# Latent attention: the mask is added by VectorE while it takes the row minimum into SBUF, and the transposes follow two tiles behind

## The chip, the cores and the metric

The kernel runs on one core of one Trainium2 chip. TensorE (PE) multiplies matrices from SBUF into PSUM; VectorE (DVE), ScalarE (ACT) and GpSimd (POOL) work beside it, each in the order of its own queue, and wait for one another through semaphores. The metric is the device time of one execution in microseconds, as the median of several runs.

## The reference, cut to what matters

The program runs four layers. The last two (`second_block`, one layer after the other) each hold a latent attention over 1024 tokens with 8 heads; this is what the change touches:

```python
def mla(q_lat, kv_lat, k_rope, ...):
    ...
    sc = (einsum('bqhd,bkhd->bhqk', qn, k_nope)       # 64 features a head
          + einsum('bqhd,bkd->bhqk', qp, k_pe)) * scale  # 32 rotated features, one key for all heads
    mask = key_chunk[None, :] <= q_chunk[:, None]     # chunks of 64 tokens
    sc = where(mask, sc, -inf)
    p = softmax(sc, axis=-1)
    return einsum('bhqk,bkhe->bqhe', p, v)
```

A query sees all keys of its own chunk of 64 and of the chunks before it. In a tile of 128 queries that leaves one corner to be hidden: the first 64 queries don't see the last 64 keys of the tile's own 128.

## The kernel before, in words

`latent_attention` is one stage between two barriers of all engines. It runs over 4 pairs of heads (p), and in each over 8 tiles of 128 queries (i); tile u = 8p + i has (i + 1) x 128 keys. The two heads of a pair are the two sides. The queries are scaled by a negative factor, so that the scores are negated, the row *minimum* is taken and the exponential is exp(minimum - score).

PSUM has 8 banks. Each side owns two banks for its scores (`s_bank`); a tile with i < 4 fills one of them (the even tiles the first, the odd ones the second), a longer one both. Three banks (`t_bank`) go round for transposes: each group of transposes takes the next bank and waits until the group three before it has been copied out (`begin`, `emptied`, `KEEP` = 3). The last bank gathers the values (`o_bank`).

All four score banks are held until the exponentials have read them: `scores` waits on "probs_ready". One step n of the loop on each engine is:

- PE: `scores(n)`: the 64-feature products (L3456), the rotated products (L3463), then for each side a product of one row by one row that adds 1e30 to the hidden corner (L3469, `early` and `late`). Then `turn(n-1)`: the probabilities of the tile before are transposed (L3484) in groups of up to four blocks. A long tile has the groups full0, full1 and then diag, or diag0 and diag1. Then pieces of other work: the queries of the next pair (`turn_q`, i = 2 and 4), the products with the values (`triangle_values`, `full_values`, L3489) and the spreading of the inverse sums (`spread`, L3510).
- DVE: a row minimum from PSUM for each side (L3603), then its share of copying out the groups (full1, diag1), the copies of the next pair's queries (i = 2 and 4: two, then four instructions), and at i = 0 and 5 the weighing of the output (`weigh`).
- ACT: copies out the first of its groups (full0), then takes the two exponentials (L3631, from PSUM to `probs`, with the row sums), then copies its other group (diag or diag0).

`probs` has two buffers. The order of all groups is written out in `LatentGroups.listed`.

The same form of instruction that the change brings in stands already in the neighbourhood attention of the first layer (L804): `tensor_tensor_reduce` from PSUM and an SBUF bias into `na_probs`, with exponentials in place behind it (L819).

Of the kernel before, what the change touches and what calls it, by code (L numbers as in the profile page):

```python
# [3327 lines left out]
class LatentGroups:  # L3328


    KEEP = 3

# [20 lines left out]
    def listed(self):  # L3353
        for part in range(4):
            yield ("q", 0, part), 1 - part % 2
        for n in range(4 * TILES + 8):
            p, i = divmod(n, TILES)
            if 1 <= n <= 4 * TILES:
                u = n - 1
                for a, what in enumerate(self.of_tile(u % TILES)):  # L3360
                    yield ("turn", u, what), 1 - a % 2
            if p < 3 and i in (2, 4):
                for part in range(2):
                    yield ("q", p + 1, (i - 2) + part), 0
            if 1 <= p <= 4 and i == 0:
                yield ("inv", p - 1, 0), 0
            if 1 <= p <= 4 and i == 5:
                yield ("inv", p - 1, 1), 0


def latent_attention(nc, core, Qn, Qr, knT, krT, V, gate, mixT):
# [9 lines left out]
    probs = [m.at("mla_probs", W + 62 * KB, [P, 2, SEQ]), m.at("mla_probs", W + 109 * KB, [P, 2, SEQ])]  # L3381
# [4 lines left out]
    low = m.at("mla_low", X + 30 * KB, [P, U, 2])  # L3386
    sums = m.at("mla_sums", X + 30 * KB + 256, [P, PAIRS_, 2, 2, 4])
    inv = m.at("mla_inv", X + 30 * KB + 512, [P, PAIRS_, 2, 2, 4])
    early = m.at("mla_early", X + 31 * KB, [P, P], F32R)
    late = m.at("mla_late", X + 31 * KB + 512, [P, P], F32R)  # L3390
# [10 lines left out]
    def scores_of(u, side):  # L3401

        i = u % TILES
        flat = s_bank[side].rearrange("p b n -> p (b n)")
        at = (i % 2) * BANK if i < 4 else 0
        return flat[:, at:at + (i + 1) * P]
    with stage(nc, "scores_ready", "lows_ready", "probs_ready", "groups_ready", "emptied_dve", "emptied_act", "inverted", "values_ready",
               "weighed", "masks_ready") as (block, s):
# [8 lines left out]
        def _(pe):  # L3417
# [18 lines left out]
            def scores(u):  # L3436
                p, i = divmod(u, TILES)
                if i == 0:
                    for part in range(4):
                        emptied(pe, ("q", p, part))  # L3440
                if u == 0:
                    pe.wait_ge(s["masks_ready"], 2)
# [7 lines left out]
                for b in range((i + 4) // 4):  # L3450
                    n = min(BANK, (i + 1) * P - b * BANK)
                    at = i % 2 if i < 4 else b
                    cols = slice(b * BANK, b * BANK + n)
                    for side in range(2):
                        rows = slice(side * NOPE, (side + 1) * NOPE)
                        pe.matmul(s_bank[side][:, at, 0:n], qnT[p % 2][rows, q], knT[rows, p, cols], start=True, stop=False)  # L3456
                for b in range((i + 4) // 4):
                    n = min(BANK, (i + 1) * P - b * BANK)
                    at = i % 2 if i < 4 else b
                    cols = slice(b * BANK, b * BANK + n)  # L3460
                    for side in range(2):
                        r0 = (2 * b + side) * ROPE
                        pe.matmul(s_bank[side][:, at, 0:n], qrT[p % 2][r0:r0 + ROPE, q], krT[r0:r0 + ROPE, cols],  # L3463
                                  start=False, stop=(b < i // 4))
                at = i % 2 if i < 4 else 1
# [5 lines left out]
                mm.then_inc(s["scores_ready"], 1)  # L3471

            def turn(u):
                i = u % TILES
                r = i % 4
                pe.wait_ge(s["probs_ready"], 2 * u + 2)
                for what in G.of_tile(i):
                    bank = begin(("turn", u, what))
                    sides = range(2) if what == "diag" else [int(what[-1])]
                    first, count = (0, 4) if what.startswith("full") else (i - r, r + 1)  # L3480
                    for a, side in enumerate(sides):
                        for k in range(count):
                            at = (a * count + k) * P
                            mm = pe.transpose(bank[:, at:at + P], probs[u % 2][:, side, (first + k) * P:(first + k + 1) * P], c["ident"])  # L3484
                    mm.then_inc(s["groups_ready"], 1)
# [30 lines left out]
            for n in range(U + 6):  # L3516
                p, i = divmod(n, TILES)
                if n < U:
                    scores(n)
                if 1 <= n <= U:  # L3520
                    turn(n - 1)
                if p < PAIRS_ - 1 and i in (2, 4):
                    for part in range(2):
                        turn_q(p + 1, (i - 2) + part)
                if p < PAIRS_ and i == 6:
                    tile_emptied(pe, n - 4)
                    tile_emptied(pe, n - 3)
# [7 lines left out]
                if p >= 1 and i == 1:  # L3535
# [4 lines left out]
                if p >= 1 and i == 2:  # L3540
                    full_values(p - 1, (2, 3))
                if p >= 1 and i == 3:
                    triangle_values(p - 1, 1, (0, 1))
                if p >= 1 and i == 4:
                    triangle_values(p - 1, 1, (2, 3)).then_inc(s["values_ready"], 1)
                if p >= 1 and i == 5:
                    spread(p - 1, 1)
# [35 lines left out]
        def _(dve):  # L3583
# [10 lines left out]
            dve.tensor_copy(early[:, :], c["early"]).then_inc(s["masks_ready"], 1)  # L3594
            dve.tensor_copy(late[:, :], c["late_big"]).then_inc(s["masks_ready"], 1)
            for part in (1, 3):
                copy_q(dve, 0, part)
            for n in range(U + 6):
                p, i = divmod(n, TILES)
                if n < U:  # L3600
                    dve.wait_ge(s["scores_ready"], n + 1)
                    for side in range(2):
                        dve.tensor_reduce(low[:, n, side:side + 1], scores_of(n, side), AX.X, ALU.min).then_inc(s["lows_ready"], 1)  # L3603
# [6 lines left out]
                if 1 <= n <= U:  # L3610
                    copy_turned(dve, n - 1, 0, slice(None))
# [3 lines left out]
                if p >= 1 and i in (0, 5):  # L3615
                    weigh(p - 1, i // 5)

        @block.scalar
        def _(act):
            for part in (0, 2):  # L3620
                copy_q(act, 0, part)
            for n in range(U + 1):
                p, i = divmod(n, TILES)
                if n >= 1:
                    copy_turned(act, n - 1, 1, slice(0, 1))
                if n < U:
                    for side in range(2):
                        act.wait_ge(s["lows_ready"], 2 * n + side + 1)
                        if n >= 2 and side == 0:
                            act.wait_ge(s["groups_ready"], G.number["turn", n - 2, G.of_tile((n - 2) % TILES)[-1]] + 1)  # L3630
                        act.activation(probs[n % 2][:, side, 0:(i + 1) * P], scores_of(n, side), ACT.Exp, bias=low[:, n, side:side + 1], scale=-1.0,  # L3631
                                       accum_out=sums[:, p, i // 4, side, i % 4:i % 4 + 1]).then_inc(s["probs_ready"], 1)
                if n >= 1:
                    copy_turned(act, n - 1, 1, slice(1, None))
# [305 lines left out]
```

## Time and profile before

| what | value |
|---|---|
| median of 3 runs | 3685.25 us (3684.77 to 3691.2) |
| span of the profiled execution | 3674.7 us, its clock 0.941 on average |
| median less that span | 10.55 us |
| PE / DVE / ACT busy, whole span | 90% / 52% / 38% |
| latent attention, first layer of the two | 2740.7 to 2909.9 us |
| latent attention, second layer of the two | 3403.1 to 3572.3 us |

The profiled execution has no time of its own beside its span; the three runs are other executions. Times within the profile are microseconds from the start of the span. Each fp32 product shows as two records on PE, each transpose as one. A duration that a timeline row gives for several instructions is that of the whole run of them; the ends on PE are modelled, so that what a piece of PE work takes is best read from its start to the start of the next one.

### The profile page before, as it was taken

The page shows a single profiled execution, that of the slowest core. Times are in us where ns is not written, and L with a number is a line of the kernel's source. Part 1 is how long each engine was busy: PE and PEld are TensorE (multiplying, and loading weights), DVE is VectorE, ACT ScalarE, POOL GpSimd, SP SyncE. Part 2 cuts the span into 40 slices and gives each one's busy share as a digit, 9 for nine tenths or more (in the row PEclk, how much of TensorE's full clock was granted, in tenths as well). Part 3 has the DMA queues.
Part 4 walks back from the last instruction along what each step waited for, and adds up shares of the span by engine and source line. Part 5 has one row for each costly group of instructions (what it writes and reads, how often), then busy time and mean ns, then how long its engine had stood idle before and what let it go on. Part 6 is the DMA issues. An engine that isn't in the chain of part 4 may idle for free. (4 is left out here: it accounts for less than half of the span.)

```text
span 3674.7 us, 49645 instructions
## 1 busy us (share of the span) xinstructions
PE 3313.7 (90%) x19127; PEld 2618.8 (71%) x19127; DVE 1919.2 (52%) x3346; ACT 1386.9 (38%) x2552; POOL 362.7 (10%) x295
## 2 busy tenths in 40 slices
PE   7999989799988989949799999799889989988899
PEld 6894457588876866737478888489755678975557
DVE  5525645566747735574547646623355443325554
ACT  2006651365744024433146646500254420024442
POOL 0100000233330000000023323100100000001000
PEclk9999989799999999969889999899789999978999
DMA  6517021587956410012358857511000221110003
GB/s 206 174 41 251 1 99 55 217 331 275 393 215 227 133 35 1 1 58 81 115 189 315 336 213 297 212 31 47 16 1 1 98 92 31 36 27 1 1 27 123
DMA packets 250401, 459.76 MB, mean 125 GB/s; under 512 B 45043, under 2 KB 120135, under 8 KB 249801
## 3 DMA queue, kind: packets, MB, share of 16 engines
q1 hardware_dynamic: 231753, 389.70, 30.1%
q0 software_dynamic: 18432, 67.12, 4.8%
q8 instruction: 143, 2.34, 0.3%
q14 instruction: 73, 0.60, 0.0%
HBM read 380.72 MB, written 73.33 MB: 124 GB/s over the span
## 5 line engine op out<-in xcount | busy, mean ns | idle before, releaser
L1774 PE MATMUL psum<-high_in,e_rowsT_high 128*128 128x256 f32 (+1 forms) x1080 | 330.3, 324 | 5.4 <-DVE e_rowsT_low L174 5.4
L1775 PE MATMUL psum<-high_in,e_rowsT_low 128*128 128x256 f32 (+1 forms) x1080 | 326.4, 320 | 0.0
L174 POOL TENSOR_TENSOR low_down<-w_down,high_out 128x1024 fp32r<-128x1024 f32 x64 | 195.5, 3071 | 312.8 <-ACT high_out L1852 312.8
L1774 PEld LDWEIGHTS psum<-high_in,e_rowsT_high 128*128 128x128 f32 x1080 | 206.7, 191 | 22.4 <-issue 6.1
L1775 PEld LDWEIGHTS psum<-high_in,e_rowsT_low 128*128 128x128 f32 x1080 | 207.0, 192 | 16.2
L3603 DVE TENSOR_REDUCE mla_low<-psum 128x1 f32<-128x256 f32 (+7 forms) x128 | 91.0, 753 | 145.7 <-PE psum L3469 145.7
L174 DVE TENSOR_TENSOR low_gate<-w_gate,high_in 128x1024 fp32r<-128x1024 f32 x128 | 148.0, 1218 | 6.5 <-ACT high_in L1852 6.5
L174 DVE TENSOR_TENSOR low_up<-w_up,high_in 128x1024 fp32r<-128x1024 f32 x128 | 148.0, 1218 | 0.0
L1852 ACT ACTIVATE high_in<-w_gate 128x1024 fp32r<-128x1024 f32 x128 | 124.8, 1058 | 60.4 <-issue 60.4
L1852 ACT ACTIVATE high_out<-w_down 128x1024 fp32r<-128x1024 f32 x128 | 124.8, 1050 | 18.8 <-DMA w_down<-in_exp_w_down 18.7
L1779 PE MATMUL psum<-low_up,e_rowsT_high 128*128 128x256 f32 x720 | 130.4, 283 | 0.0
L1852 ACT ACTIVATE high_in<-w_up 128x1024 fp32r<-128x1024 f32 x128 | 124.6, 1053 | 0.0
L1911 POOL COPY e_index<-moe_ids 128x1 uint32 (+1 forms) x49 | 9.5, 195 | 1154.3 <-POOLq L84 525.9
L156 ACT ACTIVATE proj<-psum 128x512 f32<-128x512 f32 (+2 forms) x32 | 16.9, 528 | 269.7 <-PE psum L308 229.6
L156 ACT ACTIVATE mla_probsT<-psum 128x512 f32<-128x512 f32 (+2 forms) x96 | 52.1, 543 | 173.8 <-PE psum L3484 173.8
L1798 PE MATMUL psum<-high_out,e_hiddenT_high 128*128 128x512 f32 x360 | 115.2, 401 | 0.0
L1801 PE MATMUL psum<-low_down,e_hiddenT_high 128*128 128x512 f32 x360 | 111.6, 391 | 0.0
L158 DVE COPY proj<-psum 128x512 f32<-128x512 f32 (+2 forms) x32 | 19.3, 603 | 176.4 <-PE psum L308 176.0
L1804 PE MATMUL psum<-high_out,e_hiddenT_low 128*128 128x512 f32 x360 | 111.1, 390 | 0.0
L308 PE MATMUL psum<-ring_high,s_x_low 128*128 128x512 f32 (+3 forms) x576 | 110.7, 334 | 0.0
L302 PE MATMUL psum<-ring_high,s_x_high 128*128 128x512 f32 (+3 forms) x576 | 110.7, 334 | 0.0
L306 PE MATMUL psum<-ring_low,s_x_high 128*128 128x512 f32 (+3 forms) x576 | 110.6, 334 | 0.0
(602 smaller groups left out, 7916.9 us busy)
## 6 DMA issues: line engine op xcount, KB each, us to landing
w_gate<-in_exp_w_gate SPq DMA_DIRECT2D x32, 2048.0 KB, 9.9
w_up<-in_exp_w_up SPq DMA_DIRECT2D x32, 2048.0 KB, 14.7
w_down<-in_exp_w_down SPq DMA_DIRECT2D x32, 2048.0 KB, 21.9
ada<-in_ada_w SPq DMA_DIRECT2D x24, 1024.0 KB, 7.9
expert_rows<-e_out POOLq DMA_DIRECT2D x47, 512.0 KB, 7.1
expert_rows<-zero_row SPq DMA_DIRECT2D x33, 512.0 KB, 7.0
token_rows<-x SPq DMA_DIRECT2D x32, 512.0 KB, 2.6
x<-token_rows SPq DMA_DIRECT2D x24, 512.0 KB, 6.7
```

The lines of the kernel that those rows point to most:

```text
L174: return eng.tensor_tensor(low, whole, high, ALU.subtract)
L302: pe.matmul(dst, lhsT, rhs, start=(m == 0), stop=False)
L306: pe.matmul(dst, lhsT, rhs, start=False, stop=False)
L308: mm = pe.matmul(dst, lhsT, rhs, start=False, stop=(m == len(ops) - 1))
L1774: pe.matmul(dst, rows_high[:, k, :], w_high[:, k, cols], start=(k == 0), stop=False)
L1775: pe.matmul(dst, rows_low[:, k, :], w_high[:, k, cols], start=False, stop=False)
L1779: mm = pe.matmul(dst, rows_high[:, k, :], w_low[:, k, cols], start=False, stop=(k == KT - 1))
L1798: pe.matmul(dst, hid_high[:, k, :], w_high[:, k, cols], start=(k == 0), stop=False)
L1801: pe.matmul(dst, hid_high[:, k, :], w_low[:, k, cols], start=False, stop=False)
L1804: mm = pe.matmul(dst, hid_low[:, k, :], w_high[:, k, cols], start=False, stop=(k == HT - 1))
L1852: act.activation(high(e, j)[:, k:k + STEP[j], :], W[e % 2][j][:, k:k + STEP[j], :], ACT.Copy).then_inc(s["w_high_ready"], 1)
L3603: dve.tensor_reduce(low[:, n, side:side + 1], scores_of(n, side), AX.X, ALU.min).then_inc(s["lows_ready"], 1)
```

## The change

- **The mask.** The two one-row products of each tile (L3469) go. A tile `mask` of 128 x 512 is set to zero and its last 128 columns get 1e30 for the first 64 rows. VectorE adds it while it takes the minimum.
- **The minimum.** `tensor_reduce` over a side's whole row is replaced by one `tensor_tensor_reduce` for each bank ("piece"): it reads the bank and the mask, writes the sum to `probs` in SBUF and gives the minimum. A piece without hidden columns reads one zero, broadcast. Tiles with i >= 4 have two pieces a side, and one small minimum over both (`low`, waited for by ACT through "lows_ready").
- **The score banks.** A bank is free as soon as VectorE has read it ("reduced"), not after the exponentials. PE waits for the piece two before.
- **The exponentials** read `probs` in SBUF and write it in place.
- **The lag.** `probs` has three buffers; `turn`, its copies, the values, the spreading and the weighing all come one step later. In the code this is `LAG = 2` and the shifted conditions.

```diff
 class LatentGroups:
     KEEP = 3
+    LAG = 2
...
-            if 1 <= n <= 4 * TILES:
-                u = n - 1
+            if self.LAG <= n < 4 * TILES + self.LAG:
+                u = n - self.LAG
...
-            if 1 <= p <= 4 and i == 0:
+            if 1 <= p <= 4 and i == 1:
                 yield ("inv", p - 1, 0), 0
-            if 1 <= p <= 4 and i == 5:
+            if 1 <= p <= 4 and i == 6:
...
+    def pieces_of_row(u):
+        i = u % TILES
+        return [(i % 2, 0, (i + 1) * P)] if i < 4 else [(0, 0, BANK), (1, BANK, (i - 3) * P)]
...
     scores(u), PE:
-                if i >= 4 or i == 0:
-                    if u >= 1:
-                        pe.wait_ge(s["probs_ready"], 2 * u)
-                else:
-                    if u >= 2:
-                        pe.wait_ge(s["probs_ready"], 2 * (u - 1))
+                pieces = pieces_of_row(u)
+                for b, (at, k0, n) in enumerate(pieces):
+                    if pieces_before(u) + b >= 2:
+                        pe.wait_ge(s["reduced"], 2 * (pieces_before(u) + b - 1))
...
-                for side in range(2):
-                    r0 = (2 * (i // 4) + side) * ROPE
-                    row = slice(r0, r0 + 1)
-                    mm = pe.matmul(s_bank[side][:, at, (i % 4) * P:(i % 4 + 1) * P], early[row, :], late[row, :],
-                                   start=False, stop=True)
...
     loop, PE (the turned tile and all that follows it, one step later):
-                if 1 <= n <= U:
-                    turn(n - 1)
+                if G.LAG <= n < U + G.LAG:
+                    turn(n - G.LAG)
...
-                if p < PAIRS_ and i == 6:
+                if p < PAIRS_ and i == 7:
...
                     triangle_values(p, 0, (0, 1, 2))
-                if p < PAIRS_ and i == 7:
-                    triangle_values(p, 0, (3,)).then_inc(s["values_ready"], 1)
                 if p >= 1 and i == 0:
+                    triangle_values(p - 1, 0, (3,)).then_inc(s["values_ready"], 1)
+                if p >= 1 and i == 1:
                     spread(p - 1, 0)
...
     DVE:
+            def reduce_row(u):
+                i = u % TILES
+                if u >= NP:
+                    dve.wait_ge(s["groups_ready"], G.number["turn", u - NP, G.of_tile((u - NP) % TILES)[-1]] + 1)
+                for b, (at, k0, n) in enumerate(pieces_of_row(u)):
+                    dve.wait_ge(s["scores_ready"], pieces_before(u) + b + 1)
+                    for side in range(2):
+                        hidden = mask[:, 0:1].to_broadcast([P, BANK]) if k0 + n < (i + 1) * P else mask[:, BANK - n:BANK]
+                        dst = low[:, u, side:side + 1] if i < 4 else part_low[:, u, side, b:b + 1]
+                        dve.tensor_tensor_reduce(probs[u % NP][side][:, k0:k0 + n], s_bank[side][:, at, 0:n], hidden,
+                                                 1.0, 3.0e38, ALU.add, ALU.min, dst).then_inc(s["reduced"], 1)
+                if i >= 4:
+                    dve.wait_ge(s["reduced"], 2 * pieces_before(u + 1))
+                    dve.tensor_tensor(low[:, u, :], part_low[:, u, :, 0], part_low[:, u, :, 1], ALU.min).then_inc(s["lows_ready"], 1)
...
     ACT:
-            for n in range(U + 1):
+            for n in range(U + G.LAG):
                 p, i = divmod(n, TILES)
-                if n >= 1:
-                    copy_turned(act, n - 1, 1, slice(0, 1))
+                if n >= G.LAG:
+                    copy_turned(act, n - G.LAG, 1, slice(0, 1))
                 if n < U:
                     for side in range(2):
-                        act.wait_ge(s["lows_ready"], 2 * n + side + 1)
...
+                        row = probs[n % NP][side][:, 0:(i + 1) * P]
+                        act.activation(row, row, ACT.Exp, bias=low[:, n, side:side + 1], scale=-1.0,
                                        accum_out=sums[:, p, i // 4, side, i % 4:i % 4 + 1]).then_inc(s["probs_ready"], 1)
-                if n >= 1:
-                    copy_turned(act, n - 1, 1, slice(1, None))
+                if n >= G.LAG:
+                    copy_turned(act, n - G.LAG, 1, slice(1, None))
```

## Rows read from the trace of the kernel before

**Rows 1.** The page's head: the span.

```profile
span 3674.7 us, 49645 instructions
```

**Rows 2.** Busy time by stretch: the stage in both layers, then pair 1.

```profile
core 0: us, PE busy (x) PEld busy (x) DVE busy (x) ACT busy (x) POOL busy (x), PEclk, DMA share, GB/s
2740.70:2909.92 169.22, 153.63 (x1296) 95.23 (x1296) 86.94 (x138) 72.24 (x177) 0.00 (x0) 1.00 0.00 1
3402.00:3573.00 171.00, 153.63 (x1296) 95.26 (x1297) 87.73 (x140) 73.25 (x179) 0.00 (x0) 1.00 0.00 1
...
2775.15:2816.96 41.81, 38.95 (x328) 24.10 (x329) 22.63 (x36) 17.90 (x45) 0.00 (x0) 1.00 0.00 1
```

**Rows 3.** Who waited for whom, 2740 to 2911 us (total, times, longest).

```profile
PE psum L3456 <- ACT mla_probs L3631: 13.3, 16, 1.8
...
PE psum L3484 <- ACT mla_probs L3631: 0.8, 1, 0.8
...
PE psum L3489 <- DVE mla_tmp L3589: 0.4, 1, 0.4
```

**Rows 4.** Timeline of pair 1's last two tiles: start, duration, instruction, idle before.

```profile
2806.63 1.53 PE L3484 MATMUL psum<-consts,mla_probs 128*128 128x128 f32 x12
...
2810.07 1.99 PE L3456 MATMUL psum<-mla_knT,mla_qnT 64*128 64x512 f32 x8 [0.45 <-ACT mla_probs L3631]
2811.99 1.14 PE L3463 MATMUL psum<-mla_krT,mla_qrT 32*128 32x512 f32 x8
2812.56 0.63 PE L3469 MATMUL psum<-mla_late,mla_early 1*128 1x128 f32 x2
2813.12 1.89 PE L3484 MATMUL psum<-consts,mla_probs 128*128 128x128 f32 x14
2813.22 2.35 DVE L3603 TENSOR_REDUCE mla_low<-psum 128x1 f32<-128x1024 f32 x2 [3.68 <-PE psum L3469]
2813.81 0.60 ACT L156 ACTIVATE mla_probsT<-psum 128x512 f32<-128x512 f32 x1 [3.31 <-PE psum L3484]
2814.48 1.11 ACT L3631 ACTIVATE mla_probs<-psum,mla_low 128x1024 f32<-128x1024 f32 x1
2814.94 1.09 PE L3489 MATMUL psum<-mla_probsT,mla_v 128*64 128x128 f32 x16
...
2815.61 1.11 ACT L3631 ACTIVATE mla_probs<-psum,mla_low 128x1024 f32<-128x1024 f32 x1
...
2816.72 0.48 ACT L156 ACTIVATE mla_probsT<-psum 128x384 f32<-128x384 f32 x1
2816.96 0.49 PE L3456 MATMUL psum<-mla_knT,mla_qnT 64*128 64x128 f32 x4 [0.93 <-ACT mla_probs L3631]
...
2817.86 0.88 PE L3484 MATMUL psum<-consts,mla_probs 128*128 128x128 f32 x6
```

**Rows 5.** Neighbourhood attention, first layer: L804 and L819 (ns min/median/max).

```profile
L804 DVE CUSTOM_DVE_ANT_0 na_probs<-psum,na_bias x96: 683/691/693, 280.2 to 476.3; 128x512 f32<-128x512 f32 x96
L804 DVE DVE_READ_ACCUMULATOR2_ANT na_low<- x96: 81/82/84, 280.8 to 476.9; 128x1 f32 x96
...
L819 ACT ACTIVATE na_probs<-na_probs,na_low x96: 705/722/724, 280.9 to 477.0; 128x512 f32<-128x512 f32 x96
```

**Rows 6.** Groups with their shapes apart, 2740 to 2911 us.

```profile
L3631 ACT ACTIVATE mla_probs<-psum,mla_low 128x512 f32<-128x512 f32 x8 | 5.4, 684 | 0.0
L3603 DVE TENSOR_REDUCE mla_low<-psum 128x1 f32<-128x512 f32 x8 | 5.2, 686 | 11.2 <-PE psum L3469 11.2
...
L3603 DVE TENSOR_REDUCE mla_low<-psum 128x1 f32<-128x128 f32 x8 | 2.0, 286 | 5.3 <-PE psum L3469 5.3
...
L3606 DVE RECIPROCAL mla_inv<-mla_sums 128x8 f32<-128x8 f32 x4 | 0.8, 192 | 0.0
```

**Rows 7.** The same view, 2600 to 2740 us: an operand broadcast along the row.

```profile
L3304 DVE TENSOR_TENSOR proj<-proj,mla_ms 128x1024 f32<-128x1024 f32 x1 | 1.2, 1226 | 0.0
```

**Rows 8.** Timeline of pair 0: the copies of the next queries.

```profile
2755.74 2.78 DVE L159 TENSOR_SCALAR mla_qrT<-psum 64x512 f32<-64x512 f32 x4
```

More of the change, by code:

```diff
@@ L3380, in latent_attention @@
     qrT = [m.at("mla_qrT", W + 28 * KB, [P, SEQ]), m.at("mla_qrT", X + 26 * KB, [P, SEQ])]
-    probs = [m.at("mla_probs", W + 62 * KB, [P, 2, SEQ]), m.at("mla_probs", W + 109 * KB, [P, 2, SEQ])]
+    probs = [[m.at("mla_probs", at, [P, SEQ]) for at in pair] for pair in
+             ((W + 62 * KB, W + 66 * KB), (W + 109 * KB, W + 113 * KB), (core.const_end - 4 * KB, core.const_end + 4 * KB))]
+    NP = len(probs)
     TRI = 10 * P
@@ L3385, in latent_attention @@
     tmp = m.at("mla_tmp", W + 74 * KB, [P, BANK])
[L3386 to L3390, printed above, removed]
+    low = m.at("mla_low", W + 76 * KB, [P, U, 2])
+    sums = m.at("mla_sums", W + 76 * KB + 256, [P, PAIRS_, 2, 2, 4])
+    inv = m.at("mla_inv", W + 76 * KB + 512, [P, PAIRS_, 2, 2, 4])
+    part_low = m.at("mla_part_low", W + 117 * KB, [P, U, 2, 2])
+    mask = m.at("mla_mask", X + 30 * KB, [P, BANK])
     s_bank = [core.psum[:, 0:2, :], core.psum[:, 2:4, :]]
@@ L3399, in triangle, with pieces_before, combined_before @@
         return r * (r + 1) // 2 * P
-    def scores_of(u, side):
+    def pieces_of_row(u):
         i = u % TILES
[L3404 to L3408, printed above, removed]
+        return [(i % 2, 0, (i + 1) * P)] if i < 4 else [(0, 0, BANK), (1, BANK, (i - 3) * P)]
+    def pieces_before(u):
+        p, i = divmod(u, TILES)
+        return 12 * p + (i if i < 4 else 4 + 2 * (i - 4))
+    def combined_before(u):
+        p, i = divmod(u, TILES)
+        return 4 * p + max(i - 4, 0)
+    with stage(nc, "scores_ready", "mask_steps", "reduced", "lows_ready", "probs_ready", "groups_ready", "emptied_dve", "emptied_act", "inverted", "values_ready",
+               "weighed") as (block, s):
         def emptied(eng, key):
@@ L3454, in scores @@
+                for b, (at, k0, n) in enumerate(pieces):
+                    if pieces_before(u) + b >= 2:
+                        pe.wait_ge(s["reduced"], 2 * (pieces_before(u) + b - 1))
                     for side in range(2):
                         rows = slice(side * NOPE, (side + 1) * NOPE)
[L3456 to L3460, printed above, removed]
+                        pe.matmul(s_bank[side][:, at, 0:n], qnT[p % 2][rows, q], knT[rows, p, k0:k0 + n], start=True, stop=False)
@@ L3461, in scores @@
+                for b, (at, k0, n) in enumerate(pieces):
                     for side in range(2):
                         r0 = (2 * b + side) * ROPE
-                        pe.matmul(s_bank[side][:, at, 0:n], qrT[p % 2][r0:r0 + ROPE, q], krT[r0:r0 + ROPE, cols],
-                                  start=False, stop=(b < i // 4))
-                at = i % 2 if i < 4 else 1
-                for side in range(2):
-                    r0 = (2 * (i // 4) + side) * ROPE
-                    row = slice(r0, r0 + 1)
-                    mm = pe.matmul(s_bank[side][:, at, (i % 4) * P:(i % 4 + 1) * P], early[row, :], late[row, :],
-                                   start=False, stop=True)
@@ L3471, in scores @@
-                mm.then_inc(s["scores_ready"], 1)
+                        mm = pe.matmul(s_bank[side][:, at, 0:n], qrT[p % 2][r0:r0 + ROPE, q], krT[r0:r0 + ROPE, k0:k0 + n],
+                                       start=False, stop=True)
+                    mm.then_inc(s["scores_ready"], 1)
             def turn(u):
@@ L3483, in turn @@
                             at = (a * count + k) * P
-                            mm = pe.transpose(bank[:, at:at + P], probs[u % 2][:, side, (first + k) * P:(first + k + 1) * P], c["ident"])
+                            mm = pe.transpose(bank[:, at:at + P], probs[u % NP][side][:, (first + k) * P:(first + k + 1) * P], c["ident"])
                     mm.then_inc(s["groups_ready"], 1)
@@ L3515, in _ @@
                 turn_q(0, part)
-            for n in range(U + 6):
+            for n in range(U + 7):
                 p, i = divmod(n, TILES)
@@ L3539, in _ @@
                     full_values(p - 1, (0, 1))
-                if p >= 1 and i == 2:
+                if p >= 1 and i == 3:
                     full_values(p - 1, (2, 3))
-                if p >= 1 and i == 3:
+                if p >= 1 and i == 4:
                     triangle_values(p - 1, 1, (0, 1))
-                if p >= 1 and i == 4:
+                if p >= 1 and i == 5:
                     triangle_values(p - 1, 1, (2, 3)).then_inc(s["values_ready"], 1)
-                if p >= 1 and i == 5:
+                if p >= 1 and i == 6:
                     spread(p - 1, 1)
@@ L3592, in weigh @@
                 dve.tensor_tensor(mixT[:, p, cols], tmp[:, :], t_bank(("inv", p, half)), ALU.mult).then_inc(s["emptied_dve"], 1)
-            dve.tensor_copy(early[:, :], c["early"]).then_inc(s["masks_ready"], 1)
-            dve.tensor_copy(late[:, :], c["late_big"]).then_inc(s["masks_ready"], 1)
+            def reduce_row(u):
[12 more added lines that the diff above has]
+                    dve.tensor_tensor(low[:, u, :], part_low[:, u, :, 0], part_low[:, u, :, 1], ALU.min).then_inc(s["lows_ready"], 1)
+            dve.memset(mask[:, :], 0.0).then_inc(s["mask_steps"], 1)
             for part in (1, 3):
                 copy_q(dve, 0, part)
-            for n in range(U + 6):
+            dve.wait_ge(s["mask_steps"], 1)
+            dve.tensor_copy(mask[0:CHUNK_2, BANK - P:BANK], c["late_big"][0:CHUNK_2, :]).then_inc(s["mask_steps"], 1)
+            dve.wait_ge(s["mask_steps"], 2)
+            for n in range(U + 7):
                 p, i = divmod(n, TILES)
                 if n < U:
-                    dve.wait_ge(s["scores_ready"], n + 1)
-                    for side in range(2):
-                        dve.tensor_reduce(low[:, n, side:side + 1], scores_of(n, side), AX.X, ALU.min).then_inc(s["lows_ready"], 1)
+                    reduce_row(n)
                 if p < PAIRS_ and i == 6:
@@ L3609, in _ @@
                     dve.reciprocal(inv[:, p - 1, 1, :, :], sums[:, p - 1, 1, :, :]).then_inc(s["inverted"], 1)
-                if 1 <= n <= U:
-                    copy_turned(dve, n - 1, 0, slice(None))
+                if G.LAG <= n < U + G.LAG:
+                    copy_turned(dve, n - G.LAG, 0, slice(None))
                 if p < PAIRS_ - 1 and i in (2, 4):
@@ L3614, in _ @@
                         copy_q(dve, p + 1, (i - 2) + part)
-                if p >= 1 and i in (0, 5):
-                    weigh(p - 1, i // 5)
+                if p >= 1 and i in (1, 6):
+                    weigh(p - 1, i // 6)
         @block.scalar
```

17 lines of the change are left out of this document (6 added, 11 removed).

## The prediction

> **What bounds the kernel now.** The change lives in two stages of some 170 us each, the latent attention of the last two layers; nothing outside them is touched, so I read those stretches only. The busy times by stretch come first [rows 2]. In the first layer's stage, from the first score product to the last output write, PE is busy 153.6 of 169.2 us at a granted clock of 1.00, DVE 86.9, ACT 72.2, and no transfer is under way. The second layer's stretch shows the same 153.63 us of PE. So PE sets the time, and what there is to win is its idle 15.6 us a layer and whatever work is taken off it. The waits say what the idle is made of [rows 3]: 13.3 us in 16 waits of the score products (L3456) for ACT's exponentials, 0.8 us of the last transposes for the last exponentials, 0.4 us of the values for the weighing. That is 14.5 us.
>
> The timeline of pair 1's last tiles shows how such a wait arises [rows 4]. Tile 7's scores are done when DVE starts at 2813.22. DVE needs 2.35 us for two minima, ACT takes the exponentials at 2814.48 and 2815.61, and only then are the banks free for the next scores, at 2816.96. PE meanwhile has the transposes of tile 6 and some values, and runs dry 0.93 us before. Pair 1 takes 41.8 us and has 2.86 us of such idle in all.
>
> **The change part by part.**
>
> *The mask products off PE.* Tile 7's pair of them starts at 2812.56 while the rotated products still stream; tiles 4 to 6 have theirs beside the rotated products of another bank. Sixteen transposes of 128 columns follow one another at (1.89 - 0.33)/14, some 0.11 us each [rows 4]. The two mask products have as many columns and run side by side, so together they cost at most 0.11 us, at least nothing, and I take 0.055. They are uncovered in five tiles of eight: 20 x 0.055 = 1.1 us a layer (0 to 2.2).
>
> *The new minimum.* The same instruction stands in the neighbourhood attention: 691 ns for 128x512 from PSUM with an SBUF operand, then 82 ns of accumulator read that the next instruction overlaps [rows 5]. The old minimum of that shape takes 686 ns, at 128 columns 286 [rows 6], so about 153 ns is fixed. A multiplication by an operand broadcast along the row takes 1226 ns for 1024 columns [rows 7], so the broadcast zero should cost nothing. A tile with i < 4 costs what it did. A long one pays the fixed part twice more and a small minimum over the pieces, which I price as the reciprocal, 0.19 us [rows 6], with some 0.1 us of waiting for the accumulator. That adds about 0.4 us for each of 16 tiles, 6.4 us a layer on DVE, which then has 93 of 169 us: no bound by sum.
>
> The Trainium skill ("VectorE: DVE Perf Modes", the section on the TRN2 errata) prices an SBUF-to-SBUF operation at 58 cycles plus its columns, 0.06 us for the small minimum; by it the sum would fall by about 1.3 us over both layers. The row of the reciprocal decides here.
>
> *The exponentials from SBUF.* 722 ns against 684 from PSUM at 512 columns [rows 5, 6]: 0.04 us more each, 0.08 a tile. But for a long tile ACT now starts only when both sides and the small minimum are done: for tile 7 that is 4 pieces at about 0.61, plus 0.3, plus 0.1 to begin with, so 2.9 us after the scores, where it was 1.4 (2813.12 to 2814.48).
>
> *The banks freed by DVE.* PE's wait for a score bank now ends when DVE has read the piece two before. After tile 7 that is 1.3 us, not 3.8 (2813.12 to 2816.96). PE has between two score blocks the transposes and more, so the 13.3 us go, except in one place. In pair 0 at i = 4 the DVE still has four copies of the next queries in front of it, 2.78 us [rows 8], and no values lie on PE yet to cover them. The step times, counted from tile 0's start: a product block takes 0.21 us and 0.214 for each 128 columns (1.92 for tile 7's L3456, twice 0.42 for tile 0), the rotated one at most that of 512, so scores 0 to 6 take 0.85, 1.28, 1.7, 2.1, 2.3, 2.55 and 2.8; a group of transposes takes 0.11 a block and some 0.15 once. Scores 4 then end at 10.3. DVE takes 1.65 and 0.3 for tile 4, copies one group of tile 2 (0.55) and then the four queries, and reads tile 5 only at 15.7. PE has transposes (tile 2, queries, tile 3) and scores 5, 5.2 us, to 15.5; scores 6 get their first bank at 15.7 + 1.2 + 0.1 = 17.0. Stall: 1.5 us, and 0.1 more at scores 4.
>
> *The lag, and the ring of three.* Transposes of tile n - 2 never wait for exponentials any more, but they do wait for the three transpose banks, and ACT copies the last group of a tile only behind the exponentials. I followed the steps of a steady pair with these durations, and 1.0 us for spreading, 1.9 for each half of the full values. From scores 2 at 0 on, the scores of tiles 3 to 7 and 0 begin at 4.9, 9.4, 14.4, 19.5, 24.7 and 30.7; DVE is done with tiles 2 to 7 at 2.8, 8.4, 13.8, 19.3, 24.9 and 30.5, ACT's exponentials at 3.8, 9.5, 15.5, 21.2, 27.1 and 32.9. Everything is ready when PE comes to it, with margins of 0.2 us and up, except at i = 0. From the end of scores 7, ACT's exponentials begin at +2.9, last 2 x 1.17, and end at +5.2. The copy of tile 5's diag group, four blocks (0.60), is done at +5.8. Tile 6's third group needs that bank, so it starts at +5.9. PE has as cover: transposes of tile 5 and the values, from 2806.63 to 0.45 before 2810.07, 2.99 us; scores 0, 0.85 us (2816.96 to 2817.86 less the mask); and two groups of four transposes, 0.86 [rows 4]. That is 4.75 with one hand-over, so PE stalls 1.15 us. The fourth group needs tile 6's first one copied, which ACT does next, by +6.4: another 0.25 us. So 1.4 us at this place, where 0.93 stood.
>
> It comes after tile 7 of pairs 0, 1 and 2: 4.2 us. After pair 3 there are no scores 0 to cover 0.85 of it: 2.25 us. With 1.6 us in pair 0 and 0.4 us in the tail, where the values still wait for the weighing, the new stalls are 8.45 us a layer.
>
> *At no cost.* The zeroing and copying of `mask` at the stage's start lie under the transposes and copies of the first queries, before any scores; if that cover were gone, two instructions of at most 0.7 us (by the 691 ns of 512 columns) [rows 5] would stand there once a layer. The three buffers and the longer loop issue nothing more; the same groups, values and weighings move one step down, and PE does them in the tail as before. No DMA is issued or moved.
>
> **The sum.** A layer gains 14.5 - 8.45 + 1.1 = 7.15 us; both 14.3. The profiled execution goes from its span of 3674.7 [rows 1] to 3660.4 us. The median of the runs is 10.55 us above that span, so I predict 3671 us.
>
> **The rivals.**
>
> *All idle goes.* If ACT's copies come sooner than I reckon, or PE's other work covers them, a layer wins 14.5 + 1.1, both 31 us: 3654 us. For it speaks that one step of lag is worth 5 to 6 us of PE work; against it the +5.9 to 4.75 above, of which none is a guess larger than 0.3 us. The Trainium skill ("Perfetto Trace Analysis", Optimizing Tensor Performance) advises to rotate independent groups through PSUM banks, so that their evacuation overlaps the next products; by this rule freeing the score banks alone would bring that 31 us. It doesn't bear on who empties the transposes' ring.
>
> *Nothing measurable.* The places with margins of 0.2 to 0.6 us (tile 7's fourth group at i = 1, tile 5's second and third at i = 7) turn into stalls of about 0.5 us too: three a pair, twelve a layer, 6 us of the 7.15. Then 3683 us. Against it: the steady tiles of before repeat to 0.01 us, so nothing jitters.
>
> *Slower: a dear minimum.* The instruction has been seen at one shape, 512 columns with a full second operand. If the pieces with broadcast or short operands run at half its rate, the four pieces of tile 7 take 2.4 us more, all of it on the chain scores, minimum, exponentials, copy, transpose; those of tiles 5 and 6 1.8 and 2.1. The stalls at i = 0 grow by 2.4 each (9.6 a layer), and i = 6 and 7 open by about 1.3 a pair (5): 14.6 - 7.15 = 7.5 us a layer lost, 3700 us. It decides from about 1.5 us more on that chain, 0.37 us a piece. Against it: the 5 ns between 691 and 686, and the broadcast row [rows 5 to 7].
>
> **How the numbers follow.** Forecast 0.56, all idle gone 0.14, nothing measurable 0.2, slower 0.1. The likeliest is 3671 us. The range has to reach to the second and third cases: 3655 to 3685 leaves out the slower one and little more. A measurement of this kernel tells about 0.2%, 7.4 us, from no change. Faster by more takes the first two and a little of the third: 0.74. Within: 0.17. Slower: 0.09.
>
> **What would show it.** The waits of L3456 for the exponentials gone; waits of L3456 for DVE's new instruction only in pair 0, near 1.5 us. Transposes (L3484) waiting for ACT's copies into `mla_probsT` once a pair, some 1.2 us and 0.25. New minima of 0.69 us at 512 and 0.29 at 128 columns; DVE near 93 us a stage; PE busy about 152.5 of 162. Exponentials of 512 columns at 0.72. I'd be wrong if the new instruction's short or broadcast form is dearer than the row of 512, if a held bank stops PE at more places than i = 0, or if PE's pieces take longer in their new order.

## The result and the profile after

The changed kernel takes 3659.4 us (median of 6 runs, 3655.2 to 3670.1), the kernel before in the same sets of runs 3681.7 us. The ratio is 0.995, with a 95% interval of 0.9936 to 0.9964: some 18 us faster, between 13 and 24 (the two medians lie 22.3 us apart). The forecast was 14.3 us.

What the change is worth is better read inside the two stages, whose lengths agree between the two layers to 0.01 us in both kernels. From here on the **stage** is the latent attention from the first score product to the end of the last output write. First the busy times by stretch of the changed kernel: the stage in the first layer, in the second, and pair 1.

```profile
core 0: us, PE busy (x) PEld busy (x) DVE busy (x) ACT busy (x) POOL busy (x), PEclk, DMA share, GB/s
2738.71:2899.18 160.47, 152.71 (x1232) 89.32 (x1232) 93.60 (x283) 75.23 (x177) 0.00 (x0) 1.00 0.01 1
3390.59:3551.06 160.47, 152.71 (x1232) 89.32 (x1232) 93.61 (x283) 75.23 (x177) 0.00 (x0) 1.00 0.01 1
2766.03:2805.69 39.66, 38.59 (x314) 22.66 (x312) 24.29 (x74) 18.58 (x44) 0.00 (x0) 1.00 0.01 1
```

Both stages went from 169.2 to 160.47 us [rows 2], together 17.5 us less. Pair 1 went from 41.81 to 39.66. The spans of the two profiles, 3674.7 and 3653.5, lie 21.2 us apart; the 3.7 us that the stages don't explain lie in parts that the change doesn't touch, and single runs of one kernel scatter by more than that.

Next the waits of the first layer's stage: who waited for whom, total, times, longest.

```profile
PE psum L3476 <- ACT mla_probsT L156: 4.7, 4, 1.6
...
PE psum L3457 <- DVE mla_part_low L3596: 1.7, 2, 1.4
...
PE psum L3481 <- DVE mla_tmp L3581: 0.5, 1, 0.5
```

The 13.3 us of score products waiting for exponentials [rows 3] are gone. PE waits in two new places: four times before transposes (L3476) for ACT's copies of earlier groups, and twice before scores (L3457) for DVE. With 0.5 us for the weighing that is 6.9 us against 14.5, so the waits give 7.6 of the 8.7 us that a layer gains. The other 1.1 us are about what the mask's products took (experiment 3).

The timeline around the end of pair 1 shows the first of the new waits (start, duration, instruction, idle before).

```profile
2802.77 1.53 PE L3476 MATMUL psum<-consts,mla_probs 128*128 128x128 f32 x12
2802.98 0.69 DVE L3596 CUSTOM_DVE_ANT_0 mla_probs<-psum,mla_mask 128x512 f32<-128x512 f32 x1 [0.89 <-PE psum L3461]
...
2804.23 1.53 PE L3481 MATMUL psum<-mla_probsT,mla_v 128*64 128x128 f32 x24
...
2805.55 0.16 DVE L3600 TENSOR_TENSOR mla_low<-mla_part_low 128x2 f32<-128x2 f32 x1
...
2805.69 0.49 PE L3457 MATMUL psum<-mla_knT,mla_qnT 64*128 64x128 f32 x4
2805.75 1.15 ACT L3641 ACTIVATE mla_probs<-mla_probs,mla_low 128x1024 f32<-128x1024 f32 x1 [1.69 <-DVE mla_low L3600]
...
2806.53 1.09 PE L3476 MATMUL psum<-consts,mla_probs 128*128 128x128 f32 x8
...
2806.90 1.13 ACT L3641 ACTIVATE mla_probs<-mla_probs,mla_low 128x1024 f32<-128x1024 f32 x1
...
2808.03 1.06 ACT L156 ACTIVATE mla_probsT<-psum 128x512 f32<-128x512 f32 x2
...
2808.66 1.03 PE L3476 MATMUL psum<-consts,mla_probs 128*128 128x128 f32 x6 [1.03 <-ACT mla_probsT L156]
...
2809.14 0.31 PEld L3476 LDWEIGHTS psum<-consts,mla_probs 128*128 128x128 f32 x3 [0.18 <-ACT mla_probsT L156]
...
2809.61 1.09 PE L3481 MATMUL psum<-mla_probsT,mla_v 128*64 128x128 f32 x16
```

Read it from the scores of tile 7, done at 2802.77. ACT starts its first exponential only at 2805.75, 3.0 us later, and is free at 2808.03, 5.3 us after the scores. Then it copies two groups in a row: tile 5's last and tile 6's first. PE transposed eight blocks of tile 6 from 2806.53 on and stood until the first of these copies was out: 1.03 us. A second, shorter stop is hidden inside the last group of six: the weight load for its fourth block (the PEld row at 2809.14) waited 0.18 us for the second copy. From the first of the fourteen transposes to what follows them takes 3.08 us here (2806.53 to 2809.61) and 1.92 us in experiment 8, which has no stop there. So the place costs 1.16 us, somewhat more than its wait row says.

The groups with their shapes apart, in the same stage, give the prices.

```profile
L3596 DVE CUSTOM_DVE_ANT_0 mla_probs<-psum,mla_mask 128x512 f32<-128x512 f32 x48 | 30.9, 688 | 37.9 <-PE psum L3461 37.8
...
L3641 ACT ACTIVATE mla_probs<-mla_probs,mla_low 128x512 f32<-128x512 f32 x8 | 5.7, 710 | 0.0
...
L3596 DVE CUSTOM_DVE_ANT_0 mla_probs<-psum,mla_mask 128x128 f32<-128x128 f32 x16 | 4.0, 287 | 2.3 <-PE psum L3461 2.3
...
L3600 DVE TENSOR_TENSOR mla_low<-mla_part_low 128x2 f32<-128x2 f32 x16 | 2.6, 161 | 0.6
```

### The profile page after: what moved, and what is told of

Read it like the earlier page. It is cut to its first block and busy times, and to the rows that moved or that the text cites. A ratio compares the mean times of both kernels' runs of the same rounds, so it can differ in the third digit from the quotient of the medians.

```text
span 3653.5 us, 49677 instructions
## 1 busy us (share of the span) xinstructions
PE 3304.2 (90%) x18999; PEld 2599.5 (71%) x18999; DVE 1933.3 (53%) x3634; ACT 1392.5 (38%) x2552; POOL 360.9 (10%) x295
## 5 line engine op out<-in xcount | busy, mean ns | idle before, releaser
L3596 DVE CUSTOM_DVE_ANT_0 mla_probs<-psum,mla_mask 128x512 f32<-128x512 f32 (+2 forms) x192 | 96.9, 555 | 99.3 <-PE psum L3461 99.1
L3641 ACT ACTIVATE mla_probs<-mla_probs,mla_low 128x256 f32<-128x256 f32 (+7 forms) x128 | 97.9, 766 | 47.9 <-DVE mla_low L3600 45.3
```

Source lines behind the costliest of these rows:

```text
L3641: act.activation(row, row, ACT.Exp, bias=low[:, n, side:side + 1], scale=-1.0, accum_out=sums[:, p, i // 4, side, i % 4:i % 4 + 1]).then_i ...
```

## The experiments

All start from the changed kernel, with the edits shown, and all are read by the stage of the first layer (160.47 us for the changed kernel). Four of them take the gain apart, four go after the stalls that are left.

**1. The banks held until the exponentials.** The lag of two tiles stays, but the scores wait as before:

```diff
 def scores(u):
+    if i >= 4 or i == 0:
+        if u >= 1:
+            pe.wait_ge(s["probs_ready"], 2 * u)
+    else:
+        if u >= 2:
+            pe.wait_ge(s["probs_ready"], 2 * (u - 1))
```

> The changed kernel, except that the score products of a tile again wait for the exponentials of the tile before (for the short tiles 1 to 3: of two tiles before), as in the kernel before. The measure is the length of the first layer's latent attention, from the first score product to the last output write: 169.2 us before, 160.5 changed. If the early release of the banks is what took PE's waits away, each long tile now stalls by chain less cover: tile 4 about 0.5 us, 5: 1.2, 6: 1.6, 7: 2.4, the next tile 0: 2.3, some 8 us a pair against 1.0 now, so about 188 us and a kernel near 3713 us. If the lag of two tiles alone brought the gain, the stage stays at 160 to 164 us.

The kernel takes 3757.7 us, the stage 211.05. The busy times of that stage:

```profile
2739.37:2950.42 211.05, 170.57 (x1232) 98.61 (x1232) 93.58 (x283) 75.90 (x177) 0.00 (x0) 0.90 0.00 1
```

And the end of pair 1 in its timeline, start, duration, instruction, idle before:

```profile
2818.32 1.77 PE L3463 MATMUL psum<-mla_knT,mla_qnT 64*128 64x512 f32 x8 [1.68 <-ACT mla_probs L3647]
...
2826.01 1.99 PE L3463 MATMUL psum<-mla_knT,mla_qnT 64*128 64x512 f32 x8 [2.50 <-ACT mla_probs L3647]
...
2834.60 0.59 PE L3463 MATMUL psum<-mla_knT,mla_qnT 64*128 64x128 f32 x4 [2.61 <-ACT mla_probs L3647]
...
2835.85 2.91 PE L3482 MATMUL psum<-consts,mla_probs 128*128 128x128 f32 x14
```

The stalls of this pair are the expected ones: 0.22 and 1.42 at tiles 4 and 5, then 1.68, 2.50 and 2.61 us, where 0.5, 1.2, 1.6, 2.4 and 2.3 were worked out. With the banks held, the rest of the change is thus worse than the kernel before. This run has the lag and the new minimum together, whose pieces make the exponentials come later; no run has the lag with the old minimum. But the stage is 23 us longer than expected. Some 4.5 us of it are more stalls than reckoned (39.5 us in all), and some 18 go with the clock. The granted clock is 0.90 over this stage, not 1.00, and PE's busy time for the same 1232 instructions is 170.6 us, not 152.7. The last row shows it: 14 transposes in 2.91 us after a stall, where the kernel before took 1.89 [rows 4].

**2. A lag of one tile**, the banks still freed by DVE:

```diff
-    LAG = 2
+    LAG = 1
...
-                if p < PAIRS_ and i == 7:
-                    tile_emptied(pe, n - 5)
-                    tile_emptied(pe, n - 4)
+                if p < PAIRS_ and i == 6:
+                    tile_emptied(pe, n - 4)
+                    tile_emptied(pe, n - 3)
...
-                if p >= 1 and i in (1, 6):
-                    weigh(p - 1, i // 6)
+                if p >= 1 and i in (0, 5):
+                    weigh(p - 1, i // 5)
```

(and so on for all conditions that the change had shifted).

> The changed kernel with the transposes one tile behind again, and all that follows them as before; the banks are still freed by the minimum. If the banks bring the gain and the lag only moves the last stall, transposes of tile 7 wait for the exponentials: chain 5.2 us, cover 3.75, 1.6 us for three pairs and 2.4 after the last, with about 2 us in pair 0: a stage of about 163 us against 160.5. If the lag is what carries the gain, the stage is at 169 us or above.

3667.5 us in one run, the stage 164.22 us, 164.26 in the second layer. The transposes wait five times for exponentials:

```profile
PE psum L3476 <- ACT mla_probs L3641: 7.6, 5, 2.5
...
PE psum L3457 <- DVE mla_qrT L159: 1.6, 1, 1.6
...
PE psum L3457 <- DVE mla_part_low L3596: 0.9, 1, 0.9
```

(The middle row stands before the stage.) Of the 8.7 us that a layer gains, 5.0 come without the second tile of lag (the mask's products are in them), and the second tile brings 3.7. By the rows of waits, 8.5 us here against 6.9, it should bring 1.6. The rest is in the main the clock. At the end of pair 2 the same 16 transposes that take 2.00 us elsewhere took 3.60 (the rows stand in the last section), and over the stage's last 14 us the granted clock was 0.88. By the starts of the instructions the two places lose some 3 us. What the second tile of lag saves at full clock is then nearer 1 us a layer than 3.7, an estimate from these times.

**3. The mask back on PE**, every minimum with a broadcast zero:

```diff
+                    if last:
+                        for side in range(2):
+                            r0 = (2 * b + side) * ROPE
+                            mm = pe.matmul(s_bank[side][:, at, (i % 4) * P:(i % 4 + 1) * P], early[r0:r0 + 1, :], late[r0:r0 + 1, :],
+                                           start=False, stop=True)
...
-                        hidden = mask[:, 0:1].to_broadcast([P, BANK]) if k0 + n < (i + 1) * P else mask[:, BANK - n:BANK]
+                        hidden = mask[:, 0:1].to_broadcast([P, n])
```

> The changed kernel with the mask's one-row products back on PE and a broadcast zero as the operand of every minimum. By my price of 0.055 us in five tiles of eight the stage grows by 1.1 us, from 160.5 to 161.6 us (2.2 us at most). If the products cost the time that their own records show (0.3 to 0.6 us a tile), it grows by 6 us or more. The minima with broadcast operands throughout keep their durations (0.69 us at 512 columns, 0.29 at 128) if a broadcast costs nothing.

3660.3 us in one run; the stage is 162.83 us, 2.4 more. But up to the scores of the last tile it is 0.78 us behind (139.41 against 138.63 us from the stage's start), 0.17 in each steady pair. The other 1.6 us fall in the tail, behind the last product of the mask. Its busy times, to be set against 1.00 in the same stretches of the changed kernel:

```profile
2737.00:2877.00 140.00, 134.80 (x1108) 81.76 (x1108) 83.07 (x258) 67.90 (x162) 0.00 (x0) 1.00 0.01 1
2877.00:2890.00 13.00, 11.38 (x96) 7.95 (x93) 6.91 (x19) 7.44 (x14) 0.00 (x0) 0.91 0.01 2
2890.00:2901.00 11.00, 9.29 (x98) 6.61 (x96) 4.16 (x7) 0.61 (x2) 0.00 (x0) 0.95 0.00 0
```

The 0.8 us are what is left after a stall has absorbed a part. Pair 1's end in this run:

```profile
2805.15 0.49 PE L3459 MATMUL psum<-mla_knT,mla_qnT 64*128 64x128 f32 x4
...
2806.06 1.09 PE L3486 MATMUL psum<-consts,mla_probs 128*128 128x128 f32 x8
...
2808.06 1.03 PE L3486 MATMUL psum<-consts,mla_probs 128*128 128x128 f32 x6 [0.91 <-ACT mla_probsT L156]
```

Scores 0 take 0.91 us to the next transposes, 0.84 in the changed kernel (2805.69 to 2806.53), and the stall behind them is 0.91 us in place of 1.03. Step by step, tiles 0 to 3 and 7 are each 0.06 to 0.07 us longer than in the changed kernel, tiles 4 to 6 not at all. So the mask's products cost PE some 1.2 us a layer, within 0 to 2.2 and near the 1.1 taken. The minima keep their times, 688 ns at 512 columns and 288 for 287 at 128: a broadcast operand costs nothing.

**4. A dear minimum.** A second, unused minimum in front of each piece:

```diff
+                        dve.tensor_reduce(again[:, u, side, b:b + 1], s_bank[side][:, at, 0:n], AX.X, ALU.min)
                         dve.tensor_tensor_reduce(probs[u % NP][side][:, k0:k0 + n], s_bank[side][:, at, 0:n], hidden,
```

> The changed kernel with a second, unused row minimum in front of each piece, so that each piece costs about twice as much on DVE (0.6 us more at 512 columns, 0.2 at 128). This is the price that the prediction gave to its slower case: 14.6 us a layer more than forecast, a stage of about 175 us and a kernel slower than before. DVE's sum would then be near 135 us, still less than the stage, so a view by busy sums alone expects under 165 us.

3733.2 us, the stage 195.02 us: slower than before by 26 us a layer, and 20 us more than the 175 expected. Its waits:

```profile
PE psum L3458 <- DVE mla_part_low L3598: 14.3, 18, 3.1
...
PE psum L3477 <- DVE mla_probsT L158: 6.7, 4, 2.3
...
PE psum L3477 <- ACT mla_probsT L156: 6.0, 4, 1.6
```

DVE is busy 137 of 195 us, so no sum of busy times would show a bound, and PE still stalls 29 us, 22 more than in the changed kernel where 14.6 were expected. The expectation counted the exponentials' chain only. It missed that PE now waits 18 times for DVE to free a score bank, and for DVE's own copies too. PE's busy time is 12 us longer besides, of which the granted clock of 0.95 accounts for some 10.

**5. ACT copies first.** Both of ACT's groups of a tile before the exponentials:

```diff
-                    copy_turned(act, n - G.LAG, 1, slice(0, 1))
+                    copy_turned(act, n - G.LAG, 1, slice(None))
...
-                if n >= G.LAG:
-                    copy_turned(act, n - G.LAG, 1, slice(1, None))
```

> The changed kernel with ACT copying both of its groups of a tile before it takes the exponentials, not one before and one behind. The stall at i = 0 (1.03 us three times, 1.62 in the tail) has two parts: tile 5's last group copied behind tile 7's exponentials, and tile 6's first group behind that. This edit takes away only the first part: tile 6's third group can go, the fourth still waits until the exponentials and one copy are done. Expected: 0.3 us less at each of four places, a stage of about 159.3 us against 160.5. If only the late copy of tile 5's group mattered, all 4.7 us go: 155.8 us.

3653.7 us in one run; stage 158.52 us where 159.3 was expected, the transposes' wait 3.4 us for 4.7.

```profile
2808.16 1.42 PE L3476 MATMUL psum<-consts,mla_probs 128*128 128x128 f32 x11
2810.28 0.55 PE L3476 MATMUL psum<-consts,mla_probs 128*128 128x128 f32 x3 [0.70 <-ACT mla_probsT L156]
2810.76 1.09 PE L3481 MATMUL psum<-mla_probsT,mla_v 128*64 128x128 f32 x16
```

Tile 5's last group no longer stands in the way, tile 6's first one still does: PE stops once, after eleven blocks, not after eight. The fourteen blocks take 2.60 us for 3.08, so the place gives back 0.48 us and not the 0.3 expected from the wait rows alone; four times that is about the 1.95 us gained.

**6. The same, with the engines of tile 6's first two groups changed over:**

```diff
-                    yield ("turn", u, what), 1 - a % 2
+                    yield ("turn", u, what), (0, 1, 1, 0)[a] if u % TILES == 6 else 1 - a % 2
```

> As the run with ACT's copies first, and in tile 6 the first and the second group change engines, so that DVE, which is free there, copies the first. Then nothing that PE needs at i = 0 stands behind tile 7's exponentials: the whole stall of 4.7 us a layer goes, a stage of 155.8 us (up to 157 if the other order opens a small wait). If the ring of three banks is too small whatever the order of the copies, the stall stays near 1 us a pair and the stage near 160 us.

3646.7 us in one run; stage 155.04 us. No wait of transposes for ACT is left, and the stage is 5.4 us shorter, 0.7 more than the rows of that wait add up to. The three banks are enough; which engine copies what, and in what order, made the stall.

**7. One query group copied by ACT:**

```diff
-                    yield ("q", p + 1, (i - 2) + part), 0
+                    yield ("q", p + 1, (i - 2) + part), int(i == 4 and part == 0)
...
+                if p < PAIRS_ - 1 and i == 4:
+                    copy_q(act, p + 1, 2)
```

> The changed kernel with one of the two query groups at i = 4 copied by ACT, so that DVE has two such copies in front of tile 5's minima, not four. If those four copies are what stops PE at tiles 6 and 7 of pair 0 (1.39 and 0.28 us), both waits go and the stage is 158.8 us against 160.5; pairs 1 and 2 keep their 39.7 us. If pair 0 waits for lack of other PE work, whatever DVE does there, its waits stay.

3655.6 us in one run; stage 159.57 us. The wait for DVE falls from 1.7 to 0.8, with at most 0.5 at once. Moving two of the four copies took half of it away, not all as the first branch of the expectation had it. The rest, 0.50 us at tile 6 and an unchanged 0.28 at tile 7, may be that pair 0 has no values to fill PE: pairs 1 and 2 have the same copies, and values, and no such wait. But two copies are still in front of tile 5's minima, and a run without any was not made.

**8. Both,** experiments 6 and 7 together:

> The two edits together: ACT's copies first with the engines of tile 6's first two groups changed, and one query group on ACT. Expected: 4.7 and 1.7 us less in each layer, a stage of 154.1 us, PE idle some 0.5 us in it, and a kernel 12.8 us below the changed one: about 3647 us, 0.991 of the kernel before. If the two stalls shift into one another or PE's pieces have gaps that don't show as waits, the stage stays above 156 us.

3645.1 us (median of 4 runs, 3644.1 to 3646.4) against 3679.2 for the kernel before; ratio 0.9906, interval 0.989 to 0.9923. The stage and pair 1:

```profile
2740.85:2895.00 154.15, 151.91 (x1232) 89.40 (x1232) 89.36 (x277) 79.92 (x183) 0.00 (x0) 1.00 0.01 1
2767.27:2805.76 38.49, 38.44 (x314) 22.68 (x312) 22.87 (x72) 20.11 (x46) 0.00 (x0) 1.00 0.01 1
```

And the fourteen transposes at the end of pair 1, now in one run:

```profile
2806.60 1.99 PE L3476 MATMUL psum<-consts,mla_probs 128*128 128x128 f32 x14
2808.52 1.09 PE L3481 MATMUL psum<-mla_probsT,mla_v 128*64 128x128 f32 x16
```

PE is idle 0.05 us in pair 1, and the stage is what was expected, 154.1 us. This version beats both kernels; its interval lies below that of the change, each taken against the kernel before in its own set of runs.

## Why the prediction was right

**The bound and the idle.** PE set the time, and the gain came out of its 14.5 us of waits, as predicted: 6.9 us are left. With the banks held (experiment 1) the changed kernel's stage is 42 us longer than before, some 18 of them with the clock, and with the early release but without the second tile of lag it is 5.0 us shorter: the early release is what the lag needs, not the other way round.

**The stalls at i = 0.** Predicted 1.4 us three times and 2.25 in the tail, for tile 5's last group and tile 6's first standing behind tile 7's exponentials. The wait rows say 1.03 and 1.62, 4.7 us in place of 6.45. The mechanism held by experiments 5 and 6, which take its two parts away one by one; and experiment 6 gave back 5.4 us, so that the wait rows are too small and the forecast was off by 1.0 us, not 1.7. Chain (exponentials out at +5.3 us for +5.2) and first stop (1.03 us for 1.15) were reckoned well. The second stop was there too, but shorter than the 0.25 us taken: at most 0.13 us, the 1.16 that the place costs less the 1.03. No wait row has it, since it falls inside a run of transposes. After pair 3 the place costs 2.00 us by the same reading (3.93 us from 2883.25 to 2887.18, against 1.93 in experiment 6), for the 2.25 predicted.

**The stall in pair 0.** Predicted 1.6 us for four query copies in front of tile 5's minima, measured 1.39 at scores 6, for 1.5, and 0.28 at scores 7, where none was predicted; the 0.1 at scores 4 did not show. Experiment 7 gives the copies at least half of it (0.9 us); the missing cover, which the prediction named too, may be the rest.

**The prices.** The minimum 688 ns at 512 columns and 287 at 128, as forecast from the neighbourhood attention's row; the small minimum 161 ns for the 190 taken; the exponentials 710 ns for 722. The prediction's estimate of 0.06 us, from the 58 cycles plus columns of the Trainium skill ("VectorE: DVE Perf Modes", section on the TRN2 errata), is not what this trace shows. The same section of the Trainium skill says that this row comes out too low and gives (N + 151)/0.96 ns for an fp32 `tensor_tensor` add, an estimate of 0.16 us at two columns; with that the trace agrees. DVE's sum was 93.6 us for the 93 forecast. The mask's products cost 1.2 us a layer (experiment 3) for the 1.1 taken. That figure rested on (1.89 - 0.33)/14, which is 0.11 us a transpose for the fourteen of the row, not sixteen as the prediction says.

**The sum.** Predicted 7.15 us a layer, measured 8.7: 7.6 of waits and 1.2 of mask, which is 8.8. That the two add up so closely is partly luck, since the wait rows missed 0.7 of the 5.4 us that experiment 6 gave back. Over two layers it is 17.5 us for 14.3. Of the 1.6 us a layer between the two, 1.0 is the stalls at i = 0, taken too large. The rest was not taken apart; but the forecast counted as idle the 14.5 us of its wait rows, where its own busy row left 15.6 [rows 2, 3].

The kernel's own time is the weaker witness. The median came out at 3659.4 us for the 3671 forecast, nearer to the 3654 of *all idle goes*; only the stages and their waits tell the two apart. Of these 11.5 us, 3.5 are that the kernel before took 3681.7 us in these runs and not 3685.25, 3.2 are the stages, and 4.8 are neither. The 10.55 us that were added for "median less span" are no fixed cost: every run on record takes 1.6 to 1.7 us more than its own span. The other 9 are that the profiled execution of the kernel before was a short one; from its own time the same sum gives 3662 us.

**The rivals.** *All idle goes* asked for 15.6 us a layer, and experiment 8 brought 15.05; the prediction's objection holds: it needs other copies, not this change. The Trainium skill ("Perfetto Trace Analysis", Optimizing Tensor Performance) advises to rotate independent groups through banks, so that emptying one overlaps the products of the next. The score banks agree, as no wait for exponentials is left on them; but the transposes' ring rotates too, and PE waited 4.7 us for it until the copies came in another order. *Nothing measurable*: the thin margins held, no wait opened where 0.2 us were left. *A dear minimum*: the mechanism is real and undersized by me. Doubled, it cost 34.6 us a layer over the changed kernel, not 14.6 over the forecast: 22 of stalls, since PE also waits for DVE on the score banks and for its copies, and 12 of longer busy time.

## What to carry to other kernels

When a bank or buffer is freed earlier, follow each engine's queue to the next thing that the busy engine will ask of it: here the copies that stood behind the exponentials became the wait, and putting them in front, with one pair of copies changed over between two engines, was worth 5.4 us a layer, six tenths of what the change itself brought, for no added work. Compare chain and cover at each step in microseconds; sums of busy time show neither this stall nor the one that a dearer minimum makes with DVE at 70%. And take apart a change of several edits before keeping them: without the early release, all the rest of this one loses 83 us (3757.7 against 3674.5, one run each).

## What the runs showed that I had not expected

A stall of PE can cost more than its length. With stalls of up to 3.5 us at the long tiles (experiment 1) the granted clock fell below full speed for parts of the stage, 0.66 in the worst stretch of 20 us, and PE's busy time grew by 18 us for the same instructions. In experiment 2, PE stopped 1.65 us before the same 16 transposes at the end of pairs 0, 1 and 2; they took 2.00 us twice and 3.60 us the third time. In experiment 3 one stall of 1.62 us in the tail was followed by 16 transposes in 3.29 us; in the changed kernel a stall of the same 1.62 us at the same place was followed by the same 16 in 2.00 us. So a stall of that length may or may not bring the clock down, and what decides it was not tried.

The three places in experiment 2's timeline:

```profile
2772.29 2.00 PE L3476 MATMUL psum<-consts,mla_probs 128*128 128x128 f32 x16 [1.65 <-ACT mla_probs L3641]
...
2812.39 2.00 PE L3476 MATMUL psum<-consts,mla_probs 128*128 128x128 f32 x16 [1.64 <-ACT mla_probs L3641]
...
2852.51 3.60 PE L3476 MATMUL psum<-consts,mla_probs 128*128 128x128 f32 x16 [1.65 <-ACT mla_probs L3641]
```

Experiment 1's busy times in that stretch of 20 us; PE's granted clock is the column behind POOL:

```profile
2760.00:2780.00 20.00, 13.12 (x52) 5.43 (x50) 5.86 (x21) 5.56 (x11) 0.00 (x0) 0.66 0.00 0
```

The tail in experiment 3's timeline:

```profile
2885.99 1.03 PE L3486 MATMUL psum<-consts,mla_probs 128*128 128x128 f32 x6 [1.62 <-ACT mla_probsT L156]
...
2888.26 3.29 PE L3486 MATMUL psum<-consts,mla_probs 128*128 128x128 f32 x16
```

The same in the changed kernel's:

```profile
2886.21 1.03 PE L3476 MATMUL psum<-consts,mla_probs 128*128 128x128 f32 x6 [1.62 <-ACT mla_probsT L156]
...
2888.20 2.00 PE L3476 MATMUL psum<-consts,mla_probs 128*128 128x128 f32 x16
```

In each of the two, the first row is the work right behind the stall, the last one the turn of tile 7.
